# A two-layer decoder trunk on one core: the delta-rule scan in 64x64 products by head, its output norm moved, the attention mask in PSUM, x loaded first

## The reference

```python
for l in range(DEPTH):
    x = x + 0.5 * swiglu(rms_norm(x, norm_w[l, 0]), ...)
    h = rms_norm(x, norm_w[l, 1])
    x = x + (mixer_mla_gdn(h, ...) if l % 2 == 0 else mixer_spatial_gating(h, ...))
    x = x + 0.5 * swiglu(rms_norm(x, norm_w[l, 2]), ...)

# attention, per head: softmax of the masked scores of 128-query blocks
sc = einsum('bhqd,bhkd->bhqk', q_blk, kh) * scale
p = softmax(where(key_idx <= q_idx, sc, -inf));  y_mla = einsum('bhqk,bhkd->bhqd', p, vh)

# gated delta rule, per head, 4 chunks of 64 positions, after the triangular solve for u, w
def step(state, xs):
    u_i, w_i, a_i, qd_i, kt_i, gl_i = xs
    v_new = u_i - w_i @ state
    o_i = qd_i @ state + a_i @ v_new
    state = state * exp(gl_i) + kt_i.T @ v_new
o = rms_norm(o, out_norm) * silu(z)
return concat([y_mla, o]) @ w_out
```

## Time and profile before

| | before |
|---|---|
| median of 3 runs | 1201.76 us (1200.02 to 1202.88) |
| the profiled execution | 1201.37 us |
| its span, first to last instruction | 1199.5 us |
| PE busy in the span | 1115.4 us (93%) |
| DVE, ACT busy | 669.6 us, 502.8 us |
| granted TensorE clock, mean | 0.954 |

### The profile page before, as it was taken

One profiled execution on the slowest core, in us unless ns is written; L12 is line 12 of the kernel. 1 busy time (PEld: TensorE's weight loads), 2 busy tenths in 40 slices (PEclk: granted clock), 3 DMA queues, 4 the chain that ended last, 5 costly groups with the idle time before them and its releaser, 6 DMA issues.

```text
span 1199.5 us, 18611 instructions
## 1 busy us (share of the span) xinstructions
PE 1115.4 (93%) x8225; PEld 1012.5 (84%) x8225; DVE 669.6 (56%) x823; ACT 502.8 (42%) x593; POOL 39.7 (3%) x30
## 2 busy tenths in 40 slices
PE   6999999895849969999999999999899799999998
PEld 5999987884739858999988999987677688999987
DVE  5656534678397346655544765543654645755532
ACT  5544433575520125444434544433654524544430
POOL 1000000112000000000000000000221000000000
PEclk9999999998568879999999999999999999999999
DMA  9765554444100003765553755555445453755540
GB/s 287 234 195 189 176 185 146 129 139 161 47 1 4 2 16 120 231 196 176 181 201 111 243 179 178 194 190 175 162 140 172 145 172 105 247 193 192 176 140 36
DMA packets 126905, 184.90 MB, mean 154 GB/s; under 512 B 4173, under 2 KB 101690, under 8 KB 126698
## 3 DMA queue, kind: packets, MB, share of 16 engines
q1 hardware_dynamic: 126288, 181.97, 46.1%
q0 software_dynamic: 448, 1.71, 0.6%
q10 hardware_dynamic: 90, 0.03, 0.0%
HBM read 182.66 MB, written 1.05 MB: 153 GB/s over the span
## 4 chain that ended last, share of the span: by engine, by line
PE 82%; DVE 10%; ACT 5%; issue 1%; DMA 1%; POOL 1%; SPq 0%; ACTq 0%; DVEq 0%
PE B L1177 16%; PE B L1178 16%; PE B L1179 16%; PE B L1218 7%; PE B L1222 7%; PE B L1219 7%; DVE wlo L766 3%; PE B L1545 3%; ACT whi L409 2%; DVE arena L933 1%; PE B L1285 1%; PE B L1286 1%; PE B L1287 1%; DMA raw<-in_ffn_w_up 1%; PE B L1251 1%
## 5 line engine op out<-in xcount | busy, mean ns | idle before, releaser
L766 DVE TENSOR_TENSOR wlo<-raw,whi 128x2048 fp32r<-128x2048 f32 (+1 forms) x171 | 389.6, 2280 | 290.7 <-ACT whi L409 290.6
L409 ACT ACTIVATE whi<-raw 128x2048 fp32r<-128x2048 f32 (+1 forms) x171 | 324.0, 1905 | 395.8 <-PE B L1179 246.3
L1177 PE MATMUL B<-xTh,whi 128*128 128x256 f32 x1408 | 398.7, 283 | 6.3 <-DVE arena L933 4.7
L1178 PE MATMUL B<-xTl,whi 128*128 128x256 f32 x1408 | 397.6, 282 | 0.0
L1179 PE MATMUL B<-xTh,wlo 128*128 128x256 f32 x1408 | 397.5, 282 | 0.0
L1177 PEld LDWEIGHTS B<-xTh,whi 128*128 128x128 f32 x1408 | 267.5, 190 | 7.2 <-issue 6.7
L1178 PEld LDWEIGHTS B<-xTl,whi 128*128 128x128 f32 x1408 | 267.6, 190 | 0.0
L1179 PEld LDWEIGHTS B<-xTh,wlo 128*128 128x128 f32 x1408 | 267.5, 190 | 0.0
L1218 PE MATMUL B<-whi,hTh 128*128 128x512 f32 x352 | 140.6, 399 | 8.3 <-DVE hTl L784 6.1
L1219 PE MATMUL B<-wlo,hTh 128*128 128x512 f32 x352 | 140.0, 398 | 0.0
L1222 PE MATMUL B<-whi,hTl 128*128 128x512 f32 x352 | 111.7, 399 | 0.0
(11 more groups left out here) (235 smaller groups left out, 1049.0 us busy)
## 6 DMA issues: line engine op xcount, KB each, us to landing
raw<-in_ffn_w_up SPq DMA_DIRECT2D x44, 1024.0 KB, 5.2
raw<-in_ffn_w_down SPq DMA_DIRECT2D x44, 1024.0 KB, 4.8
raw<-in_ffn_w_gate SPq DMA_DIRECT2D x43, 1024.0 KB, 5.2
raw<-in_sg_w_in SPq DMA_DIRECT2D x16, 1024.0 KB, 5.3
raw<-in_ab_w_in SPq DMA_DIRECT2D x8, 1024.0 KB, 5.0
raw<-in_sg_w_out SPq DMA_DIRECT2D x8, 1024.0 KB, 4.8
raw<-in_ab_w_out SPq DMA_DIRECT2D x4, 1024.0 KB, 5.0
raw<-in_ab_w_in SPq DMA_DIRECT2D x2, 832.0 KB, 4.3
```

The source lines that it names most:

```text
L409: A(whi[:, j % SLOTS, 0:kt * width], raw[:, j % SLOTS, 0:kt * width], ACT.Copy).then_inc(S("hi_ready"), 1)
L766: TT(wlo[:, j % SLOTS, 0:n], raw[:, j % SLOTS, 0:n], whi[:, j % SLOTS, 0:n].bitcast(f32), ALU.subtract).then_inc(S("lo_ready"), 1)
L1177: mm(out_ap, lh, rh, start=first, stop=False)
L1178: mm(out_ap, lh, rl, start=False, stop=False)
```

## The change

1. Start: x is loaded in four quarters, the first column half of both row blocks first, then the first piece of unit 0. The identity and the norm weights go to ACT's queue, and POOL's five small broadcast loads wait until unit 0 is rounded.
2. Attention: PE adds the mask in PSUM, as a product of the identity by the mask block for two of three blocks. DVE takes the maxima and ACT the exponentials straight from PSUM; `probs` has two buffers, the scores four banks. The copy to `pT` moves from ACT to DVE.
3. The attention half of Y is transposed between the transposes of k and of decayed q (`y_transposes(0, 4)`). Its split into `hTh` and `hTl` stands on ACT after the copies of the systems, on DVE between the first and the second merge level.
4. Scan: the DT-by-v products of all four chunks go first. `state` holds 64 columns per pair of heads, and wT, qdT, kt by head are 64x64 products, the even heads on rows 0 to 63 and the odd on 64 to 127. Even heads' v goes to bank 0 and is copied by ACT, odd heads' to bank 1 and is copied by DVE. The kt products stand ahead of the AT products.
5. Way out: o stays in PSUM. ACT squares it there, DVE multiplies it by the gate from there, block t = 0 while chunk 3 still runs. PE runs the first unit of the output projection (attention columns alone), then the eight transposes of the other half, then the second unit, and only then waits for their split.

```diff
             for h in range(HEADS):                         # ACT
                 act.wait_ge(S("softmax_in"), h + 1)
-                if h:
-                    act.wait_ge(S("pT_sums"), h)
-                A(probs[:, 0, :], scores[:, 0, :], ACT.Exp, ...)
+                if h >= 2:
+                    act.wait_ge(S("pT_sums"), h - 1)
+                scores, p = B[SCORE_BANK[h % 4]][:, 0:384]..., probs[h % 2]
+                A(p[:, 0, :], scores[:, 0, :], ACT.Exp, ...)
...
-                act.wait_ge(S("pT_sums"), h + 1)
-                A(pT[:, h % 2, :], B[4][:, 0:3 * P], ACT.Copy).then_inc(S("pT_out"), 1)
...
+            row_max(0)                                     # DVE
+            row_max(1)
             for h in range(HEADS):
-                TT(scores[:, 0:2, :], src[:, 0:2, :], bc(future.unsqueeze(1), [P, 2, P]), ALU.add)
-                nc.vector.tensor_copy(scores[:, 2, :], src[:, 2, :])
...
+                dve.wait_ge(S("pT_sums"), h + 1)
+                nc.vector.tensor_copy(pT[:, h % 2, :], B[4 + h % 2][:, 0:3 * P]).then_inc(S("pT_out"), 1)
+                if h + 2 < HEADS:
+                    row_max(h + 2)
...
                 for i, (tq, tk) in enumerate(((0, 0), (1, 1), (1, 0))):      # PE
+                    last = mm(o, qTm[...], kTm[...], start=True, stop=i == 2)
+                    if i < 2:
+                        mm(o, ident, future, start=False, stop=True)
...
+                if i == 1:
+                    pe.wait_ge(S("eg_ready"), 4)
+                    pe.wait_ge(S("gc_ready"), 1)
+                    y_transposes(0, 4)
...
+            for t in range(NT):
+                for q, odd, h in heads():
+                    for r in HC:
+                        last = mm(B[odd][r, ...], DT[r, m], QKVn[2][r, t, 64 * h:64 * h + 64], ...)
             for n in range(4):
                 if n:
-                    for q in range(PAIRS):
-                        last = mm(B[0][r, P * q:P * q + P], wT[:, q, tok], state[:, q, :], ...)
+                    for q, odd, h in heads():
+                        last = mm(B[odd][r, ...], wT[HC[odd], q, tok], state[HC[odd], q, :], ...)
+                    last.then_inc(S("v_sums"), 1)
+                    for q, odd, h in heads():
+                        last = mm(B[O_BANK[t][odd]][r, ...], qdT[HC[odd], q, tok], state[HC[odd], q, :], ...)
+                pe.wait_ge(S("v_new_even"), n + 1)
+                pe.wait_ge(S("v_new_odd"), n + 1)
+                if n < 3:
+                    for q, odd, h in heads():
+                        last = mm(B[4][HC[odd], ...], kt[r, ...], v_new[r, q, odd, :], ...)
+                    last.then_inc(S("s_sums"), 1)
+                for q, odd, h in heads():
+                    last = mm(B[O_BANK[t][odd]][r, ...], AT[r, ...], v_new[r, q, odd, :], ...)
...
-            pe.wait_ge(S("y_gdn"), 1)
-            for t in range(NT):
-                for k in range(KD):
-                    last = transpose(B[X_BANK[k // 2]]..., Y[:, t, P * k:P * k + P], ident)
-            pe.wait_ge(S("yT_lo"), 8)
-            down(1, b + 12, 4)
+            pe.wait_ge(S("o_weighted"), 2)
+            down(1, b + 12, 4, upto=1)
+            pe.wait_ge(S("y_gdn"), 2)
+            y_transposes(4, 8)
+            down(1, b + 12, 4, done_before=1, upto=2)
+            pe.wait_ge(S("yT_lo"), 8)
+            down(1, b + 12, 4, done_before=2)
```

More of the change, by code:

```diff
@@ L212, in build_trunk @@
         tmp, k_sq = at(4096, 1536), at(0, NT, HEADS * NOPE)
-        scores = at(H1, 3, P)
-        probs = at(H1 + 384, 3, P)
+        probs = [at(H1 + 384 * i, 3, P) for i in range(2)]
         qm = at(6400, NT, HEADS * QK)
@@ L224, in build_trunk @@
         xc = at(R0 + 2912, 2, 2, SEQ)
[L226 removed]
+        gU, Dec, DecB, Lm, Am = [at(1024 * i, 1024) for i in range(5)]
+        LT, AT = at(R0 + 5472, 1024), at(R0 + 6496, 1024)
         kbe, kt = at(9216, 1024), at(10240, 1024)
@@ L1583, in _, with heads @@
                 last.then_inc(S("w_sums"), 1)
+            def heads(): return [(q, odd, 2 * q + odd) for q in range(PAIRS) for odd in range(2)]
+            for t in range(NT):
+                for q, odd, h in heads():
+                    m = slice(64 * (8 * t + h), 64 * (8 * t + h) + 64)
+                    for r in HC:
+                        last = mm(B[odd][r, 64 * (4 * t + q):64 * (4 * t + q) + 64], DT[r, m],
+                                  QKVn[2][r, t, 64 * h:64 * h + 64], start=(t == 0 and q == 0), stop=True,
+                                  skip_group_check=True)
+            last.then_inc(S("v_sums"), 1)
             pe.wait_ge(S("w_ready"), 4)
-            pe.wait_ge(S("state_zero"), 1)
+            pe.wait_ge(S("yT_lo"), 4)
             for n in range(4):
@@ L1601, in _ @@
-                last.then_inc(S("v_sums"), 1)
-                for q in range(PAIRS):
-                    if n:
-                        mm(B[1][r, P * q:P * q + P], qdT[:, q, tok], state[:, q, :], start=q == 0, stop=False,
-                           skip_group_check=True)
-                pe.wait_ge(S("v_new_ready"), n + 1)
-                for h in range(HEADS):
-                    last = mm(B[1][r, 64 * h:64 * h + 64], AT[r, 64 * (8 * t + h):64 * (8 * t + h) + 64],
-                              v_new[r, 64 * h:64 * h + 64], start=(n == 0 and h == 0), stop=True,
-                              skip_group_check=True)
@@ L1611, in _ @@
[L1611 to L1624 removed]
+                    pe.wait_ge(S("state_ready"), n)
@@ new lines, in _ @@
+                    for q, odd, h in heads():
+                        last = mm(B[odd][r, 64 * (4 * t + q):64 * (4 * t + q) + 64], wT[HC[odd], q, tok],
+                                  state[HC[odd], q, :], start=False, stop=True, skip_group_check=True)
+                    last.then_inc(S("v_sums"), 1)
+                    for q, odd, h in heads():
+                        last = mm(B[O_BANK[t][odd]][r, 64 * q:64 * q + 64], qdT[HC[odd], q, tok],
+                                  state[HC[odd], q, :], start=q == 0, stop=False,
+                                  skip_group_check=True)
```

231 lines of the change are left out of this document (133 added, 98 removed).

## The result

The changed kernel takes 1165.85 us (median of 4 runs, 1163.74 to 1166.77), the kernel before 1201.7 us (1200.02 to 1202.88). The ratio is 0.970, 95% interval 0.9683 to 0.9718: 35.9 us less. The forecast was 26.8 us less, 1175 us, with a range from 1166 to 1189 us. The four runs lie on both sides of that end, so on which side the median fell is luck; the 9 us are not.

What follows compares the result with a forecast made beforehand. PE, busy 1115 of 1199.5 us, was taken as the bound, with low-clock or sparse stretches in attention, scan and way out. Terms -1.5 - 4.5 + 3.1 - 23.9 = -26.8 us gave 1175 us, range 1166 to 1189.

Steps and rivals of the forecast that it cites:

- the term between attention and scan: Early Y transposes (1.7 us, half at 2.4 GHz) and DVE's four subtractions (1.4) delay PE: +3.1 us (1 to 3.1).
- Start: Kernel start: moving POOL's small loads, 2.5 us of DMA time, brings unit 1's load earlier: -1.5 us (0 to -2.5).
- Attention: Attention heads: PE enters without a long stop, the clock stays at 2.4 GHz, 2.2 us a head: -4.5 us.
- the attention stays at 1.2 GHz: Rival: the attention keeps the low clock, 9 us more than the sum, 1184 us; chance 0.20.
- Scan: From the end of w to the last AT: 12.7 us against 22.3, with smaller products and v products first.
- The chunk of 2.6 us: One scan chunk (v, copies of v, kt, serial AT) takes 2.6 us instead of 5.12.
- The 1.5 us added for a stretch at the low clock: Added to the scan's 9.3 us of chunks, because a stretch of it ran at the low clock before.
- the small products go one by one: Rival in the scan: v, qdT and kt take 1.07 us each, 14.4 us instead of 9.3, time 1180; chance 0.12.
- The case that the prediction took from the Trainium skill: Scan: weight loads overlap matmuls only in differing row groups, so kt alone is serial: 1.7 us, time 1176.5.
- Way out: Last AT to second output unit: 7.7 us against 22.0, the first output unit running while the norm takes 6.1.
- slower: Rival: clock stays at 1.2 GHz from attention to projection, merges +15.6 us, in all +4.7, 1206 us; chance 0.04.
- all clocks high: Low end of the forecast range, 1166 us; scan and way out all at 2.4 GHz give -26.1.

Runs made afterwards that it cites:

- s_start: Kernel before with the change's start alone (x in halves first, identity and norm rows from ACT's queue, POOL's small loads held back): 1199.06 us, ratio 0.9979.
- a_nomask: Changed kernel without the mask products in its attention, so its output lacks the causal mask: 1164.36 us, ratio 0.9684 to the kernel before.
- a_filler: Kernel before with 10 unread products added where PE stood still between head 1's scores and the first transposes: 1201.64 us, ratio 0.9995.
- after_again: The changed kernel measured and profiled once more, nothing altered: 1166.55 us, ratio 0.9700 to the kernel before.
- b_mix: Changed kernel with DVE's four subtractions behind the merge loop and y's early transposes one step further up: 1162.09 us, ratio 0.9665 to the kernel before.
- h_serial: Changed kernel with the heads of wT, qdT and kt ordered so that neighbours share rows and columns: 1167.35 us, ratio 0.9703 to the kernel before.
- s_hold: Kernel before with one wait added: POOL's small loads wait until unit 0 has been split: 1198.82 us, ratio 0.9964.
- b_fill: Changed kernel with y's early transposes behind the v products and 8 unread transposes in their old place: 1167.83 us, ratio 0.9705 to the kernel before.
- b_tr_late: Changed kernel with y's early transposes behind the v products, their copies and subtractions behind chunk 0: 1167.23 us, ratio 0.9704 to the kernel before.

## Why the prediction fell short, and what held

The step of the prediction that failed most is the term between attention and scan, +3.1 us, measured at -0.9: it kept the Gram products at their old price.

**Start, -1.5, measured -3.45 in the trace.** The step at fault is "if all of that lay ahead of unit 1, the chain gains 2.5 us, if none, nothing": it priced POOL's loads as DMA time. The cause named was right, the channel mostly wrong. Of the 3.45 us, 2.2 are the earlier issue of unit 1 and 0.9 the shorter issue itself (0.61 instead of 1.53); at most 0.4 is left for the transfer. The runs showed SP's issues of 0.38 to 0.61 us instead of 1.04 on average for unit 0's pieces, which the trace of before held: unit 1 was issued at 6.81 us though only 8 issues lay ahead of it. By the ratio `s_start` was worth 2.5 us (0.6 to 4.6), so a part of the 3.45 is this one profile's.

**Attention, -4.5, measured -5.96.** PE was the limit (`a_nomask`) and the clock stayed (2.07 us a head, 2.2 forecast: the 0.133 us for a score instruction at the full clock was read from a group with its own beginning and end in it; in the head's loop two take 0.22). The rows before gave 23.6 us to PE alone; that a loop of 2.91 us lay under it was left out, and left the clock alone 0.6 us to give (`a_filler`). The change broke the loop as well, so here the gap in the reasoning cost nothing, by luck. The rival "the attention stays at 1.2 GHz" did not come in any profile with the new attention.

**Between, +3.1, measured -0.88.** This term failed most, by 4.0 us. Two pieces were mis-sized. The transposes: forecast 1.7 "half that at 2.4 GHz"; the stage was 0.7 us longer in the profiled run (11.2 to 11.9) and 0.7 shorter in `after_again` (10.5), where the clock did not fall between them. The subtractions: 1.4 forecast, 0.9 to 1.2 measured. The large piece is one the sum left out: it kept the Gram products at their old price, at 1.2 GHz, though the working itself says that the clock had risen in a run of transposes ahead of the attention. The Gram products went from 5.69 us to 3.43, and the 3.1 us at 1.2 GHz behind them, which are the transposes of the systems, went too: 2.7 us in that stage by the profiles at either clock (37.6 to 34.9). With 1.0 us less for the transposes and 0.3 less for the subtractions that makes the 4.0. Three of the seven profiles without such transposes have the higher clock too, so in some runs of the kernel before this gain isn't there to be had.

The Trainium skill, "TensorE: Matmul & The Clock Gate", Part 4, says that the full clock does not engage for transposes. The trace does not agree: in the kernel before PE did nothing but transposes from 301.53 to 307.0 us, and the clock, 0.50 up to 306 us, was at 1.00 before they ended, and in `b_mix` 8 transposes of y took 1.04 us at 1.00.

**Scan, -9.6, measured -10.95.** The chunk of 2.6 us was 2.50 to 2.56. The 1.5 us added for a stretch at the low clock was not needed: 11.3 us instead of 12.7. wT went at 0.03 (0.33 for the last 12), inside its bounds; 16 took 0.63 us for qdT, 0.68 for kt and 1.11 for AT. The rival "the small products go one by one" was refuted by the changed kernel for wT and kt; `h_serial`, which brings a part of it about, paid 1.6 us in the scan. The case that the prediction took from the Trainium skill, "TensorE: Matmul & The Clock Gate", Part 3, would have kt at 1.07 us for 16. The trace does not agree: 0.68 us with shared rows, against 0.63 for qdT where they differ.

**Way out, -14.3, measured -14.7.** The norm took 6.2 us (399.43 to 405.58; forecast 6.1) and the first unit hid under it.

**The rival "slower"** needed the merges at 1.2 GHz. The five levels were at 1.00 in all 17 profiles; only the transposes of the systems ahead of them were partly at 0.50, in four.

**The sum.** The terms were off by 2.0, 1.5, 4.0, 1.4 and 0.4 us, all to one side, 9.2 with rounding; the profiled run adds 1.6 of spread. The range failed for the reason that its low end, "all clocks high", held only the scan, the way out and the attention. The between stage had no gain in it at all, and the start none above 2.5 us. Even so the best bounds of the terms, -2.5, -4.5, +1 and -26.1, come to 1169 us; the 3 us below that, down to 1166, had no term behind them, and without them the miss would have been plain.

**Open:** what slows SP's issues, and why earlier with POOL's loads about; how the attention's gain splits between buffers, copy and clock; and what in the two orders of PE's work decides the clock of the Gram products, beyond that work ahead of them goes with the higher one.

## What to carry to other kernels

Before pricing a stage by its busiest engine, add up the loop that comes right after it (here 2.91 us under 3.09): a filler in the engine's idle time is a cheap test of whether its clock is what costs, if the clock of every run is looked at and not only the profiled one's. When a change adds PE work in front of a dense stretch, price that stretch at both clocks, and give the term a bound below zero. At a kernel's start read the issue times of each queue as well as the transfers: one wait that kept five small loads off for 12 us gave 4.3 us (2.8 to 5.9); the same wait with a new order of the first loads gave 2.5 (0.6 to 4.6), and the new order alone nothing.

## What the runs showed of the hardware that was not expected

- SP's first nine issues took 0.37 to 0.47 us each with POOL's queue silent (`s_hold`), the next two 2.08 and 2.60. With POOL's small loads issued in the first 4 us, slow ones came from the fifth on (0.83, then 2.04 us, in the kernel before).
- Products of 64x64 in f32 at 2.4 GHz, 16 instructions from the first's start to the last's end: 0.63 us with rows alternating and columns the same (qdT), 0.68 with rows the same and columns alternating (kt), 0.93 with runs of 8 in one quarter (kt of `h_serial`), 1.11 in one quarter alone (AT).
- With eight transposes nobody reads ahead of them the Gram products took 3.43 us instead of 5.70 (`b_fill` and `b_tr_late`, one profile each; the mean clocks of their runs agree in eight of nine), and the stage before them grew by 1.7 us.
